# One encoder layer with routed experts on one core: mixing and experts in one overlaid block, and another order of the splits inside an expert block

## The chip, the cores and the metric

The kernel runs on one core of a Trainium2 chip. The metric is the device time of one execution in microseconds (us), the median of the runs; before, three runs gave 1725.3, 1727.06 and 1738.86 us. A profile is one further execution. PE is TensorE, DVE VectorE, ACT ScalarE, POOL GpSimd and SP SyncE. SP issues DMAs on one queue, POOL on another; both run on the core's 16 DMA engines.

## The reference

Two sequences (512 and 1024 tokens of width 1024, in all 1536 tokens, 12 tiles of 128) go through one layer: a retention mixer and a latent attention side by side, one output projection with residual, and a mixture of 32 experts (4 groups of 8; top group, then the top 2 experts in it). What follows the attention is what the change touches:

```
x = x + mix @ w_out
h = rmsnorm(x, g_ffn)
g = argmax(softmax(h @ w_rg)); top 2 of softmax(h @ w_re) inside group g; share = p_group * p_top / sum(p_top)
for each block of 128 rows of one expert e:
    y = (silu(xb @ w_g[e]) * (xb @ w_u[e])) @ w_d[e]        # w_g, w_u: 1024x512, w_d: 512x1024, f32
x[token] += share * y
out = rmsnorm(x, g_final)
```

## The kernel before

Four phases follow each other: projection (names a_), latent attention (c_), mixing and routing (d_, `phase_mix`) and the experts (e_, `phase_experts`). Each has its own on-chip tensors and its own block of five instruction streams; at its end all engines meet at a barrier and its semaphores are cleared.

Every f32 product is done in three passes (lines 91 to 95): both operands are split into a high half, the value rounded by a cast on ScalarE, and a low half, the remainder by a subtraction on VectorE, and TensorE adds high x high, high x low and low x high.

**Mixing.** `phase_mix` splits w_out into d_w_hi and d_w_lo (8 slices of 128x1024, raw in d_stage) and then walks the 12 tiles by `pairs` (line 73: two tiles written out, a loop, two tiles written out). For each tile: project and add the residual (d_x, line 1735), normalise (d_h_sb, 1739), turn the rows (1639), router logits (1646), a chain of 11 small VectorE operations that picks group and experts (1747 to 1769), and one tile later the places in each expert's queue (`queue`, 1713 to 1726). POOL stores x_mid (1578) and h_rows (1581) and scatters each token's entry into `table`, which lists the rows of each expert (1590). The loop leaves VectorE idle while TensorE projects. Behind the last tile VectorE works out the gates and then counts blocks: which expert each further block has, and n_pairs, the number of pairs of blocks (1792 to 1813). POOL stores the gates as `shares` (1598). SP has issued the whole first expert's weights behind its last tile (1553).

**Experts.** An expert's gate, up and down weights are six pieces j = 0 to 5 of 128x2048 f32, 1 MB each (0 and 1 gate, 2 and 3 up, 4 and 5 down), in the single buffer `raw`. SP loads a piece once its low half of the block before is done:

```
for j in pieces:
    sp.wait_ge(s_wlo[j], n)
    sp.dma_start(raw[:, j // 2, span(j)], w_exp[j // 2][e][:, span(j)]).then_inc(s_raw[j], 16)
```

Its order is pieces 0 to 3 of block n, then 4 and 5 of block n - 1. There are 32 blocks here. `each_block` (1876) writes out blocks 0 and 1 and loops over the rest. Block n on each engine:

- TensorE (2035): gate product (e_pg), up product (e_pu), turning of block n+1's rows (e_px, 1998), first half of the output product of block n-1 (e_py), turning of block n's gated product (e_ph, 2028), second half of e_py.
- ScalarE (2088): high halves of pieces 0 and 1, high half of the turned rows (2069), pieces 2 and 3, output scaling of block n-2 (2076), pieces 4 and 5 of n-1, high half of e_ph (2086), silu (2102).
- VectorE (2154): low halves of pieces 0 and 1 (2125), gated product of n-1 (`hidden`, 2146), low half of the turned rows (2132), pieces 2 and 3, output scaling (2139), low half of e_ph (2150), pieces 4 and 5 of n-1.
- POOL (1970): gather of block n+2's rows (e_xg, 1938), list of rows of block n+3 (e_who, 1932); then it waits until the scatter of block n-2 has landed, reads the code list of block n (e_code, 1978), gathers its shares (e_gate, 1946) and issues the scatter-add of block n-1's output into x_mid (1955). All of it waits in order on POOL.

At the end x_mid is read back and normalised (2112 to 2184).

Of the kernel before, what the change touches and what calls it, by code (L numbers as in the profile page):

```python
# [28 lines left out]
P = 128  # L29
D = 1024  # L30
# [1426 lines left out]
def phase_mix(nc, mixT, x_all, w_out, w_fold, g_ffn, w_rg, w_re, ident_d, route_d, blocks_d, x_mid, h_rows, table,  # L1457
              gates, blocks, n_pairs, s_tick, s_tock, raw, s_raw0, w_exp, shares):
    with ExitStack() as ctx:
        def sb(name, shape, dt=F32):  # L1460
            return ctx.enter_context(nc.sbuf_tensor("d_" + name, shape, dt))

        sems = phase_sems(nc, ctx)

# [3 lines left out]
        ident = sb("ident", [P, P])  # L1468
        route = sb("route", [P, 2 * NE + 2 * P])
        e_id, e_grp = route[:, 0:NE], route[:, NE:2 * NE]  # L1470
        before, ones = route[:, 2 * NE:2 * NE + P], route[:, 2 * NE + P:]
        stage = sb("stage", [P, 3, D])
        w_hi, w_lo = sb("w_hi", [P, KD, D], F32R), sb("w_lo", [P, KD, D], F32R)
        w_r = sb("w_r", [P, KD, NG + NE])
        g_row = sb("g_row", [P, D])
        eps = sb("eps", [P, 1])
        mx, xr = sb("mx", [P, 2, D]), sb("xr", [P, 2, D])
        mT_hi, mT_lo = sb("mT_hi", [P, 2, D], F32R), sb("mT_lo", [P, 2, D], F32R)
        x2, h_sb, hT = sb("x2", [P, 2, D]), sb("h_sb", [P, 2, D]), sb("hT", [P, D])
        junk = sb("junk", [P, D], BF16)  # L1480
        ssq, root, rstd = sb("ssq", [P, 1]), sb("root", [P, 1]), sb("rstd", [P, 1])
        g8, g8max, e8 = sb("g8", [P, 8]), sb("g8max", [P, 8]), sb("e8", [P, 8])
        g8i, e8i = sb("g8i", [P, 8], U32), sb("e8i", [P, 8], U32)
        gf, ef = sb("gf", [P, 1]), sb("ef", [P, 2])
        mask, pen, lem = sb("mask", [P, NE]), sb("pen", [P, NE]), sb("lem", [P, NE])
        hot = sb("hot", [P, 3, NE])
        seen = sb("seen", [P, NE])
        prod = sb("prod", [P, NE])
        place, spot = sb("place", [P, 2]), sb("spot", [P, 2])
        spot_i = sb("spot_i", [P, 2, 2], I32)  # L1490
        entry = sb("entry", [P, 2, 2, 2], I32)
        empty = sb("empty", [P, NE * ROWS // P * 2], I32)
        glog, elog = sb("glog", [P, TILES, NG]), sb("elog", [P, TILES, 2])
        gm, gz, ge, gd, gr = (sb(n, [P, TILES]) for n in ("gm", "gz", "ge", "gd", "gr"))
        gx = sb("gx", [P, TILES, NG])
        many_i, many, incl = sb("many_i", [P, NE], I32), sb("many", [P, NE]), sb("incl", [P, NE])
        step_no = sb("step_no", [P, MORE + AHEAD])
        upto, uses = sb("upto", [P, MORE + AHEAD, NE]), sb("uses", [P, MORE + AHEAD, NE])
        who, gone, base = (sb(n, [P, MORE + AHEAD]) for n in ("who", "gone", "base"))

        po = [ctx.enter_context(nc.psum_tensor(f"d_po{i}", [P, 1024], F32)) for i in range(2)]
        pt = ctx.enter_context(nc.psum_tensor("d_pt", [P, 1024], F32))
        pr = ctx.enter_context(nc.psum_tensor("d_pr", [P, 512], F32))
        pp = ctx.enter_context(nc.psum_tensor("d_pp", [P, 512], F32))
# [10 lines left out]
        s_spare, s_gates = sem("spare"), sem("gates")  # L1515
        s_d, s_q, s_gexp, s_count, s_g = sem("d"), sem("q"), sem("gexp"), sem("count"), sem("g")

        block = ctx.enter_context(nc.Block())

        @block.sync  # L1520
        def _(sp):
# [27 lines left out]

            pairs(sp, TILES, tile)  # L1550

            for j in range(6):
                sp.dma_start(raw[:, j // 2, raw_span(j)], w_exp[j // 2][0][:, raw_span(j)]).then_inc(s_raw0[j], 16)

        @block.gpsimd
        def _(pool):
# [28 lines left out]
            def enter(t, half):  # L1585
# [3 lines left out]
                for c in range(2):  # L1589
# [6 lines left out]
            pool.wait_ge(s_gates, 1)  # L1596
            settle_waits(pool, s_tick)
            pool.dma_start(shares[0:2 * ROWS, :].rearrange("(t p c) a -> p t (c a)", p=P, c=2),
                           gates[:]).then_inc(s_spare, 16)
# [3 lines left out]
            pool.wait_ge(s_spare, 16)  # L1603
# [52 lines left out]
        def _(act):  # L1656
# [12 lines left out]
            def tile(r, half, last):  # L1669
# [13 lines left out]
            pairs(act, TILES, tile)  # L1683
            act.wait_ge(s_gexp, 1)
# [4 lines left out]
        def _(dve):  # L1689
# [3 lines left out]
            dve.wait_ge(s_init, 3)  # L1693
            def split(t, half):
# [13 lines left out]
            def queue(t, half, again):  # L1708
# [6 lines left out]
                for c in range(2):  # L1715
                    ins = nc.vector.tensor_reduce(place[:, c:c + 1], pen[:] if c else prod[:], AX.X, ALU.add)
                queue_steps.chain(ins)
                queue_steps.chain(nc.vector.scalar_tensor_tensor(out=spot[:], in0=ef[:], scalar=float(ROWS),
                                                                 in1=place[:], op0=ALU.mult, op1=ALU.add))
# [556 lines left out]
```

## Time and profile before

| | us |
|---|---|
| three runs | 1725.3, 1727.06, 1738.86 |
| median | 1727.06 |
| the profiled execution | 1740.69 |
| its span, first to last instruction | 1739.2 |
| projection, about 0 to 497 | 497 |
| latent attention, about 497 to 798 | 301 |
| mixing and routing, about 798 to 1040 | 242 |
| experts and final norm, about 1040 to 1739 | 699 |

The span is read in stages, since the share of busy time over all of it mixes stages with different limits. Of a stage, the windows give the busy time of each engine, the granted TensorE clock and the share and rate of DMA. The chain is followed back from the last instruction to what released it each time; "idle before" of an instruction is the time in which its engine had nothing to run, with the releaser that ended it.

### The profile page before, as it was taken

The numbers are of one execution on the slowest core, as the hardware profiler recorded it, in microseconds if no ns is written. First come the engines' busy times: TensorE is split into PE (matmuls) and PEld (weight loads), VectorE is DVE, ScalarE is ACT, GpSimd is POOL, SyncE is SP. The second block draws the span as 40 slices with busy tenths as digits, with TensorE's granted clock in tenths as the row PEclk, the third lists the DMA queues.
The fourth block names the chain that finished last, engine by engine and source line by source line (L and its number), as shares of the span: only waits on it lengthen the run. The fifth ranks groups of instructions, "written<-read, shape, count | busy, mean of one in ns | idle before, by whom it ended". The sixth has DMA issues, their size and how long they took to land. (4 is left out here: it accounts for less than half of the span.)

```text
span 1739.2 us, 21978 instructions
## 1 busy us (share of the span) xinstructions
PE 1517.8 (87%) x7474; PEld 1251.4 (72%) x7474; DVE 1091.5 (63%) x1590; ACT 841.2 (48%) x1112; POOL 323.3 (19%) x291
## 2 busy tenths in 40 slices
PE   6999999999947799994999936999999989999980
PEld 5888788888836678872788825778777768777760
DVE  5656754434335577662355545888887878888854
ACT  6433433333324454452222215777766757767734
POOL 0000111111110000000012222223333333343340
PEclk9999999999967899996999967999999999999995
DMA  7132411221132100005344526999999999999947
GB/s 241 61 97 100 138 55 61 73 67 55 37 105 73 61 25 13 19 13 170 120 145 146 215 76 240 366 379 370 377 366 346 365 320 349 361 354 365 369 134 298
DMA packets 83266, 327.17 MB, mean 188 GB/s; under 512 B 16819, under 2 KB 27203, under 8 KB 58499
## 3 DMA queue, kind: packets, MB, share of 16 engines
q1 hardware_dynamic: 63426, 278.88, 43.4%
q0 software_dynamic: 19776, 47.47, 9.4%
q8 instruction: 37, 0.61, 0.1%
q14 instruction: 27, 0.21, 0.0%
HBM read 281.83 MB, written 53.91 MB: 193 GB/s over the span
## 5 line engine op out<-in xcount | busy, mean ns | idle before, releaser
L2125 DVE TENSOR_TENSOR e_w_lo<-raw,e_w_hi 128x2048 fp32r<-128x2048 f32 x192 | 428.0, 2282 | 8.5 <-ACT e_w_hi L2064 8.5
L2064 ACT CAST e_w_hi<-raw 128x2048 fp32r<-128x2048 f32 x192 | 356.8, 1912 | 14.3 <-PEq L104 12.7
L93 PE MATMUL a_p<-a_w_hi,a_xT_hi 128*128 128x512 f32 (+1 forms) x480 | 194.8, 406 | 3.4 <-DVE a_w_lo L679 3.3
L95 PE MATMUL a_p<-a_w_hi,a_xT_lo 128*128 128x512 f32 (+1 forms) x480 | 187.4, 390 | 0.0
L94 PE MATMUL a_p<-a_w_lo,a_xT_hi 128*128 128x512 f32 (+1 forms) x480 | 186.5, 389 | 0.0
L93 PE MATMUL e_py<-e_w_hi,e_hT_hi 128*128 128x512 f32 x256 | 108.3, 423 | 8.0 <-DVE e_w_lo L2125 8.0
L93 PEld LDWEIGHTS a_p<-a_w_hi,a_xT_hi 128*128 128x128 f32 x480 | 91.4, 190 | 20.4 <-DVE a_xT_lo L673 3.7
L93 PE MATMUL e_pg<-e_w_hi,e_xT_hi 128*128 128x512 f32 x256 | 102.5, 401 | 1.8 <-DVE e_xT_lo L2132 1.8
L95 PEld LDWEIGHTS a_p<-a_w_hi,a_xT_lo 128*128 128x128 f32 x480 | 91.1, 190 | 17.9
L93 PE MATMUL d_po<-d_w_hi,d_mT_hi 128*128 128x512 f32 x192 | 81.8, 426 | 24.8 <-DVE d_w_lo L1702 24.8
L94 PE MATMUL e_py<-e_w_lo,e_hT_hi 128*128 128x512 f32 x256 | 103.0, 402 | 0.0
L95 PE MATMUL e_py<-e_w_hi,e_hT_lo 128*128 128x512 f32 x256 | 102.7, 401 | 0.0
L94 PEld LDWEIGHTS a_p<-a_w_lo,a_xT_hi 128*128 128x128 f32 x480 | 91.6, 191 | 14.9
L95 PE MATMUL e_pg<-e_w_hi,e_xT_lo 128*128 128x512 f32 x256 | 102.1, 399 | 0.0
L94 PE MATMUL e_pg<-e_w_lo,e_xT_hi 128*128 128x512 f32 x256 | 102.0, 399 | 0.0
L95 PE MATMUL e_pu<-e_w_hi,e_xT_lo 128*128 128x512 f32 x256 | 101.2, 395 | 0.0
L93 PE MATMUL e_pu<-e_w_hi,e_xT_hi 128*128 128x512 f32 x256 | 101.1, 395 | 0.0
L94 PE MATMUL e_pu<-e_w_lo,e_xT_hi 128*128 128x512 f32 x256 | 101.0, 395 | 0.0
L2076 ACT ACTIVATE e_y_sb<-e_py,e_gate 128x512 f32<-128x512 f32 x32 | 22.0, 688 | 138.4 <-PE e_py L95 80.8
L1946 POOL DMA_INDIRECT e_gate<-s_shares,e_code x32 | 59.6, 1863 | 157.9 <-DMA e_code<-s_table 146.1
L1431 DVE TENSOR_TENSOR c_pT_lo<-c_pt,c_pT_hi 128x512 fp32r<-128x512 f32 x80 | 52.2, 683 | 47.8 <-ACT c_pT_hi L1282 47.8
L2150 DVE TENSOR_TENSOR e_hT_lo<-e_ph,e_hT_hi 128x512 fp32r<-128x512 f32 x32 | 22.1, 692 | 95.1 <-ACT e_hT_hi L2086 95.1
(310 smaller groups left out, 3306.2 us busy)
## 6 DMA issues: line engine op xcount, KB each, us to landing
raw<-in_w_gate SPq DMA_DIRECT2D x64, 1024.0 KB
raw<-in_w_up SPq DMA_DIRECT2D x64, 1024.0 KB
raw<-in_w_down SPq DMA_DIRECT2D x64, 1024.0 KB
a_x_sb<-in_x SPq DMA_DIRECT2D x24, 512.0 KB, 4.0
s_mid<-a_kv SPq DMA_DIRECT2D x12, 512.0 KB, 2.9
a_kv<-s_mid SPq DMA_DIRECT2D x12, 512.0 KB, 3.5
d_mx<-s_mixT SPq DMA_DIRECT2D x12, 512.0 KB, 5.4
d_xr<-in_x SPq DMA_DIRECT2D x12, 512.0 KB, 3.7
```

The costliest lines, as they stand in the source:

```text
L93: pe.matmul(out, st_hi, mv_hi, start=first, stop=False)
L94: pe.matmul(out, st_hi, mv_lo, start=False, stop=False)
L95: return pe.matmul(out, st_lo, mv_hi, start=False, stop=last)
L1431: nc.vector.tensor_tensor(pT3_lo[:, 4 * i:4 * i + 4, j * P:(j + 1) * P], pt[:, c * 512:(c + 1) * 512].rearrange("p (k i) -> p k i", k=4), ...
L1946: pool.indirect_dma_start(out=gate[half][:], out_offset=None, in_=shares, in_offset=bass.IndirectOffsetOnAxis(ap=code[half][:, 1:2], axis= ...
L2064: nc.scalar.copy(w_hi[:, j // 2, span(j)], raw[:, j // 2, span(j)]).then_inc(s_whi[j], 1)
L2076: nc.scalar.activation(y_sb[half][:, 0:512], py[:, 0:512], ACT.Copy, scale=gate[half][:, 0:1]).then_inc(s_ya, 1)
L2125: nc.vector.tensor_tensor(w_lo[:, j // 2, span(j)], raw[:, j // 2, span(j)], w_hi[:, j // 2, span(j)].bitcast(F32), ALU.subtract).then_inc ...
L2150: nc.vector.tensor_tensor(hT_lo[:], ph[:], hT_hi[:].bitcast(F32), ALU.subtract).then_inc(s_hlo, 1)
```

## The change

Mixing and experts share one block of instruction streams: no barrier and no clearing of semaphores lies between them. For that all on-chip tensors of both lie in two arenas, `split` for the halves and `plain` for the rest, with places that overlap where one is dead before the other is written, and PSUM is one tensor `acc`. In rows of the changed kernel's order everything has these three names. New waits guard the overlap: SP issues expert 0's weights in two parts (pieces 0 to 2 behind tile 1, once w_out is split; 3 to 5 behind tile 10); VectorE waits for the cleared table before it splits w_out.

The splits of expert 0's pieces 0 to 3 move into the tail of mixing. Block 0 of the experts no longer has them. The count of blocks moves behind block 0's turned rows. POOL's clearing of e_xg is dropped, that of e_gate and the store of the shares move behind the first gathers. Inside each expert block, piece 1 is split behind the gated product and the turned rows.

```diff
+                if isinstance(r, int) and t in (1, TILES - 2):
+                    sp.wait_ge(s_wlo, KD)
+                    for j in range(3) if t == 1 else range(3, 6):
+                        sp.dma_start(raw[:, j // 2, raw_span(j)],
+                                     w_exp[j // 2][0][:, raw_span(j)]).then_inc(ex.s_raw[j], 16)
             pairs(sp, TILES, tile)
-            for j in range(6):
-                sp.dma_start(raw[:, j // 2, raw_span(j)], w_exp[j // 2][0][:, raw_span(j)]).then_inc(s_raw0[j], 16)
...
+                if last:
+                    act.wait_ge(s_po, TILES)
+                    ex.upper(nc.scalar, 0, 0)
                 for b in range(2):
                     act.wait_ge(s_ht, 2 * t + b + 1)
...
             pairs(act, TILES, tile)
+            for j in range(1, 4):
+                ex.upper(nc.scalar, j, 0)
...
+            dve.wait_ge(s_tab[1], 16)
...
+                if last:
+                    dve.wait_ge(s_x2, TILES)
+                    ex.lower(nc.vector, 0, 0)
                 if not (isinstance(t, int) and t == 0):
                     queue(t - 1, 1 - half, not (isinstance(t, int) and t == 1))
+                if last:
+                    ex.lower(nc.vector, 1, 0)
...
             nc.vector.tensor_copy(prod[:, 0:1], spot[:, 0:1]).then_inc(s_spot, 1)
+            ex.lower(nc.vector, 2, 0)
+            ex.lower(nc.vector, 3, 0)
...
+            eng.wait_ge(ex.s_pairs, 1)
             with eng.Fori(1, pair_count(eng)) as r:
...
         def _(sp):
-            sp.dma_start(ident[:], ident_d).then_inc(s_const, 16)
+            sp.wait_ge(s_normed, TILES)
             sp.dma_start(g_row[:], g_final.partition_broadcast(P)).then_inc(s_const, 16)
...
-            for half in range(2):
-                nc.gpsimd.memset(gate[half][:], 0.0)
-                nc.gpsimd.memset(xg[half][:], 0.0).then_inc(s_clear, 1)
-            pool.wait_ge(s_clear, 2)
             for n in range(2):
                 list_rows(n, start_of(n))
             for half in range(2):
                 gather_rows(0, half)
             pool.wait_ge(s_xg[0], 16)
             list_rows(0, start_of(2))
+            for half in range(2):
+                ins = nc.gpsimd.memset(gate[half][:], 0.0)
+            ins.then_inc(s_clear, 1)
+            pool.wait_ge(s_clear, 1)
+            pool.wait_ge(s_gates, 1)
+            settle_waits(pool, s_tick)
+            pool.dma_start(shares[0:2 * ROWS, :].rearrange("(t p c) a -> p t (c a)", p=P, c=2),
+                           gates[:]).then_inc(ex.s_shares, 16)
+            pool.wait_ge(ex.s_shares, 16)
...
             def step(r, half):
                 n = 2 * r + half
-                split(0, n)
-                split(1, n)
-                if not (isinstance(r, int) and n == 0):
+                again = not (isinstance(r, int) and n == 0)
+                if again:
+                    split(0, n)
                     hidden(n - 1)
                 rows_lo(n)
-                split(2, n)
-                split(3, n)
+                if again:
+                    split(1, n)
+                    split(2, n)
+                    split(3, n)
+                else:
+                    count_blocks(dve)
```

ScalarE's step has the same new order: piece 0, turned rows, pieces 1 to 3. `ex.upper` and `ex.lower` are the split of one piece on ScalarE and VectorE, with the waits of before.

What stands in a row on VectorE in one block of the experts' loop, before:

```order
L2125 TENSOR_TENSOR e_w_lo<-raw,e_w_hi 128x2048 x2
L2146 TENSOR_TENSOR e_h_sb<-e_act_g,e_pu 128x512
L2131 ISA
L2132 TENSOR_TENSOR e_xT_lo<-e_px,e_xT_hi 128x512
L2131 REGISTER_ALU
L2132 TENSOR_TENSOR e_xT_lo<-e_px,e_xT_hi 128x512
L2125 TENSOR_TENSOR e_w_lo<-raw,e_w_hi 128x2048 x2
```

and after (L1537 is the low half of a piece, L2222 the gated product, L2208 the turned rows):

```order
L1537 TENSOR_TENSOR split<-plain,split 128x2048
L2222 TENSOR_TENSOR plain<-plain,acc 128x512
L2207 ISA
L2208 TENSOR_TENSOR split<-acc,split 128x512
L2207 REGISTER_ALU
L2208 TENSOR_TENSOR split<-acc,split 128x512
L1537 TENSOR_TENSOR split<-plain,split 128x2048 x3
```

One piece has moved from ahead of the gated product to behind the turned rows.

VectorE behind the last queue places of mixing, before (L1776 is the last copy of the queue places, L1778 begins the gates, L1792 the count of blocks, L1807 to L1813 its end, L2125 pieces 0 and 1 of block 0):

```order
L1776 COPY d_prod<-d_spot 128x1
L1778 TENSOR_REDUCE d_gm<-d_glog 128x12
...
L1789 TENSOR_TENSOR gates<-d_gr,d_gd 128x12
L1792 TENSOR_SCALAR d_many_i<-d_pp 128x32
...
L1813 TENSOR_SCALAR n_pairs<-d_many_i 1x1
...
L2125 TENSOR_TENSOR e_w_lo<-raw,e_w_hi 128x2048 x2
L2132 TENSOR_TENSOR e_xT_lo<-e_px,e_xT_hi 128x512 x2
L2125 TENSOR_TENSOR e_w_lo<-raw,e_w_hi 128x2048 x4
```

and after (L1867 is the last copy, L1871 begins the gates, L1888 to L1909 is the count):

```order
L1867 COPY plain<-plain 128x1
L1537 TENSOR_TENSOR split<-plain,split 128x2048 x2
L1871 TENSOR_REDUCE plain<-plain 128x12
...
L1882 TENSOR_TENSOR plain<-plain 128x12
...
L2208 TENSOR_TENSOR split<-acc,split 128x512 x2
L1888 TENSOR_SCALAR plain<-acc 128x32
...
L1909 TENSOR_SCALAR plain<-plain 1x1
L1537 TENSOR_TENSOR split<-plain,split 128x2048
```

Pieces 2 and 3 stand ahead of the gates, and the count stands behind the turned rows of block 0.

POOL at the phase end, before (entries of the last tile, shares, clearing, first lists and gathers):

```order
L1590 DMA s_table<-d_entry,d_spot_i 49152x2 x4
L1598 DMA s_shares<-gates 128x12x2
...
L1960 MEMSET e_gate 128x1
L1961 MEMSET e_xg 128x1024
L1960 MEMSET e_gate 128x1
L1961 MEMSET e_xg 128x1024
L1932 DMA e_who<-s_table 128x2 x2
L1938 DMA e_xg<-s_h_rows,e_who 128x1024 x2
L1932 DMA e_who<-s_table 128x2
```

and after:

```order
L1674 DMA s_table<-plain 49152x2 x4
L2000 UNCONDITIONAL_BRANCH
L2010 DMA plain<-s_table 128x2 x2
L2016 DMA plain<-s_h_rows,plain 128x1024 x2
L2010 DMA plain<-s_table 128x2
L2044 MEMSET plain 128x1 x2
L2049 DMA s_shares<-plain 128x12x2
```

The lists and gathers follow the entries, and the store of the shares has moved behind them.

## Rows read from the trace of the kernel before

**Rows 1.** Windows: us, busy PE PEld DVE ACT POOL, PEclk, DMA share, GB/s.

```profile
798.00:1040.00 242.00, 190.95 (x914) 157.79 (x914) 113.47 (x420) 53.10 (x84) 40.67 (x55) 0.85 0.45 153
1040.00:1072.00 32.00, 16.08 (x60) 12.97 (x61) 13.72 (x9) 13.95 (x10) 10.11 (x13) 0.63 0.53 184
...
1100.00:1260.00 160.00, 157.82 (x724) 127.41 (x723) 141.74 (x96) 118.38 (x95) 54.28 (x41) 1.00 1.00 374
1260.00:1660.00 400.00, 375.45 (x1685) 299.96 (x1684) 328.19 (x222) 272.01 (x221) 141.80 (x101) 0.99 0.97 355
```

**Rows 2.** Page, part 4: the chain of work that ended last, by engine.

```profile
DMA 22%; issue 5%; PE 3%; DVE 3%; ACT 3%; POOLq 2%; POOL 1%; DVEq 0%; ACTq 0%; SPq 0%
```

**Rows 3.** Timeline of POOL across the phase end: start, duration, line, operation, idle before.

```profile
1028.60 0.97 POOL L1590 DMA_INDIRECT s_table<-d_entry,d_spot_i  x1 [0.30 <-issue]
...
1040.18 0.10 POOL L1960 MEMSET e_gate<- 128x1 f32 x1 [9.51 <-POOLq L104]
```

**Rows 4.** Timeline of DVE in the last mixing tile and across the phase end.

```profile
1020.21 0.16 DVE L1747 COPY d_glog<-d_pr 128x4 f32<-128x4 f32 x1 [2.19 <-PE d_pr L1646]
...
1035.12 0.13 DVE L1813 TENSOR_SCALAR n_pairs<-d_many_i 1x1 int32<-1x1 int32 x1
1040.25 0.06 DVE L2142 MEMSET e_eps<- 128x1 f32 x1 [5.00 <-PEq L104]
```

**Rows 5.** Chain in order of time, first block of the experts: start, duration, what.

```profile
1042.38 2.37 DMA e_who<-s_table
...
1045.70 8.69 DMA e_xg<-s_h_rows,e_who
...
1057.86 0.79 PE e_pg L93
```

**Rows 6.** Timeline of SP's queue: the expert weights issued in the first blocks.

```profile
1044.50 2.53 SPq L1892 DMA_DIRECT2D raw<-in_w_gate  x2
...
1071.17 2.54 SPq L1892 DMA_DIRECT2D raw<-in_w_gate  x2
```

**Rows 7.** Chain in order of time: one block of the scatter chain, and the last scatter.

```profile
1259.59 10.49 DMA s_x_mid<-e_y_sb,e_code
...
1271.44 4.70 DMA e_code<-s_table
...
1279.42 10.21 DMA s_x_mid<-e_y_sb,e_code
...
1697.07 6.27 DMA s_x_mid<-e_y_sb,e_code
```

**Rows 8.** Timeline of POOL: scatters of blocks 0, 5 and 29.

```profile
1098.38 1.66 POOL L1955 DMA_INDIRECT s_x_mid<-e_y_sb,e_code  x1 [13.46 <-DVE e_y_sb L2139]
...
1193.35 3.76 POOL L1955 DMA_INDIRECT s_x_mid<-e_y_sb,e_code  x1 [0.30 <-issue]
...
1672.96 1.65 POOL L1955 DMA_INDIRECT s_x_mid<-e_y_sb,e_code  x1 [0.30 <-issue]
```

**Rows 9.** Timeline of DVE: one expert block of the even stretch.

```profile
1155.50 0.69 DVE L2150 TENSOR_TENSOR e_hT_lo<-e_ph,e_hT_hi 128x512 fp32r<-128x512 f32 x1 [2.16 <-ACT e_hT_hi L2086]
1156.11 8.89 DVE L2125 TENSOR_TENSOR e_w_lo<-raw,e_w_hi 128x2048 fp32r<-128x2048 f32 x4
1164.91 0.68 DVE L2146 TENSOR_TENSOR e_h_sb<-e_act_g,e_pu 128x512 f32<-128x512 f32 x1
1165.51 1.28 DVE L2132 TENSOR_TENSOR e_xT_lo<-e_px,e_xT_hi 128x512 fp32r<-128x512 f32 x2
...
1174.18 0.69 DVE L2150 TENSOR_TENSOR e_hT_lo<-e_ph,e_hT_hi 128x512 fp32r<-128x512 f32 x1 [2.33 <-ACT e_hT_hi L2086]
```

**Rows 10.** Waits in 1258 to 1660: who waits for whom; total, times, longest.

```profile
PE e_ph L2028 <- DVE e_h_sb L2146: 21.2, 19, 4.1
...
ACT e_y_sb L2076 <- DMA e_gate<-s_shares,e_code: 21.9, 4, 9.0
```

**Rows 11.** Waits in 1109 to 1258: ScalarE for the gate weights.

```profile
ACT e_w_hi L2064 <- DMA raw<-in_w_gate: 0.9, 2, 0.5
```

More of the change, by code:

```diff
@@ L1454, with raw_span, __init__, at @@
 NOWHERE = 1 << 20
-def phase_mix(nc, mixT, x_all, w_out, w_fold, g_ffn, w_rg, w_re, ident_d, route_d, blocks_d, x_mid, h_rows, table,
-              gates, blocks, n_pairs, s_tick, s_tock, raw, s_raw0, w_exp, shares):
+def raw_span(j):
+    return slice(2048 * (j % 2), 2048 * (j % 2 + 1))
+KB = 1024
+SPLIT_WORDS, PLAIN_WORDS = 27648, 25536
+class Map:
+    def __init__(self, arena, start):
+        self.arena, self.next = arena, start
+    def at(self, shape, dt, offset):
+        count = 1
+        for n in shape[1:]:
+            count *= n
+        words = count * (2 if dt == BF16 else 4) // 4
+        view = self.arena[0:shape[0], offset // 4:offset // 4 + words]
+        if dt not in (F32, F32R):
+            view = view.bitcast(dt)
+        if len(shape) == 3:
+            return view.rearrange("p (a b) -> p a b", a=shape[1])
+        if len(shape) == 4:
+            return view.rearrange("p (a b c) -> p a b c", a=shape[1], b=shape[2])
+        return view
+    def add(self, shape, dt=F32):
+        count = 1
+        for n in shape[1:]:
+            count *= n
+        offset = self.next
+        self.next += (count * (2 if dt == BF16 else 4) + 31) // 32 * 32
+        return self.at(shape, dt, offset)
@@ L1497, in phase_mix @@
[L1497 to L1504, printed above, removed]
+        w_r = sb([P, KD, NG + NE])
@@ new lines, in phase_mix @@
+        entry = sb([P, 2, 2, 2], I32)
+        glog, elog = sb([P, TILES, NG]), sb([P, TILES, 2])
+        gm, gz, ge, gd, gr = (sb([P, TILES]) for _ in range(5))
+        gx = sb([P, TILES, NG])
+        many_i, many, incl = sb([P, NE], I32), sb([P, NE]), sb([P, NE])
+        step_no = sb([P, MORE + AHEAD])
+        who, gone, base = (sb([P, MORE + AHEAD]) for _ in range(3))
+        po = [acc[:, 1024 * i:1024 * (i + 1)] for i in range(2)]
+        pt = acc[:, 2048:3072]
+        pr, pp = acc[:, 3072:3584], acc[:, 3584:4096]
@@ L1514, in phase_mix @@
         s_tab = [sem("tab0"), sem("tab1")]
-        s_spare, s_gates = sem("spare"), sem("gates")
+        s_gates = sem("gates")
+        s_steps = sem("steps")
         s_d, s_q, s_gexp, s_count, s_g = sem("d"), sem("q"), sem("gexp"), sem("count"), sem("g")
-        block = ctx.enter_context(nc.Block())
         @block.sync
@@ L1812, in _ @@
             nc.vector.tensor_copy(n_pairs[:, 0:1], many_i[0:1, 0:1])
-            tail.chain(nc.vector.tensor_scalar(n_pairs[:, 1:2], many_i[0:1, 0:1], -1.0, None, ALU.add))
-def raw_span(j):
-    return slice(2048 * (j % 2), 2048 * (j % 2 + 1))
-def phase_experts(nc, w_exp, ident_d, h_rows, table, shares, blocks, n_pairs, s_tick, raw, s_raw, x_mid, g_final,
-                  out):
+            nc.vector.tensor_scalar(n_pairs[:, 1:2], many_i[0:1, 0:1], -1.0, None, ALU.add).then_inc(ex.s_pairs, 1)
@@ L1825, in phase_experts @@
+        return s_h, s_gates, count_blocks
+def phase_experts(nc, block, sems, split, plain, acc, ex, w_exp, h_rows, table, shares, s_tick, x_mid, g_final, out, gates, s_normed, s_gates,
+                  count_blocks):
     KF = FE // P
     with ExitStack() as ctx:
-        def sb(name, shape, dt=F32):
-            return ctx.enter_context(nc.sbuf_tensor("e_" + name, shape, dt))
-        sems = phase_sems(nc, ctx)
         def sem(name):
             return phase_sem(nc, sems, "e_" + name)
-        ident = sb("ident", [P, P])
@@ L1846, in phase_experts @@
[L1846 to L1848 removed]
+        ident, w_hi, w_lo, raw = ex.ident, ex.w_hi, ex.w_lo, ex.raw
+        who, code, xg, y_sb, gate = ex.who, ex.code, ex.xg, ex.y_sb, ex.gate
+        xT_hi, xT_lo, act_g, h_sb = ex.xT_hi, ex.xT_lo, ex.act_g, ex.h_sb
+        hT_hi, hT_lo, g_row, eps = ex.hT_hi, ex.hT_lo, ex.g_row, ex.eps
```

183 lines of the change are left out of this document (101 added, 82 removed).

## The prediction

> **What bounds the kernel now.** I read the windows first, then the chain that ended last, then the timelines of single engines at two places.
>
> The windows [rows 1] show four regimes behind the latent phase. In mixing (798 to 1040) the DMA share is 0.45 and TensorE is busy 191 of 242 us. From 1040 to 1072 everything is thin: TensorE 16 of 32 us, clock 0.63, DMA 0.53. From 1100 to 1260 DMA and TensorE are both full (share 1.00, 374 GB/s, TensorE 157.8 of 160 us). From 1260 to 1660 DMA stays near full (0.97, 355 GB/s), but TensorE has 24.6 us of holes.
>
> The chain [rows 2] is a DMA chain: 22% of the span, against 3% for each compute engine. Its links in the experts [rows 7] are the scatter-add of a block's output rows into x_mid (10.49 us to land), then the code list of the block after next (4.70 us), whose queueing waited for that landing, then the gather of the shares, then the next scatter, 19.83 us after the first (1259.59 to 1279.42). POOL issues all of these itself, one behind the other. After block 0, where POOL waited 13.46 us for the output, it starts a scatter with 0.30 us of idle time in front of it [rows 8], so the outputs lie ready and the chain waits only for its own transfers. Its pace is (1193.35 - 1098.38) / 5 = 19.0 us a block at first and (1672.96 - 1193.35) / 24 = 20.0 us after that [rows 8].
>
> The compute side needs less. VectorE's cycle in the even stretch is 1174.18 - 1155.50 = 18.7 us [rows 9]. In that cycle the gated product (L2146) stands behind four weight pieces (8.89 us), and the turning of h, the second half of the output product and the next scaling follow on it. So two loops run side by side: one of compute at 18.6 us and one of transfers at 19 to 20 us. The second sets the end.
>
> **Part 1: the phase end goes.** Before, the table entries of tile 11 are issued at 1028.60 [rows 3]. VectorE then counts blocks until 1035.25, the barrier and the clearing of semaphores last to 1040.25 [rows 4], and POOL clears two 128x1024 tiles. The first list of rows is read at 1042.38 [rows 5]. After the change POOL reads it as soon as the entries have landed. The trace has no landing time for that scatter, so I bound it: a list of the same 1 KB lands in 2.37 us [rows 5], the last scatter of 128 whole rows in 6.27 us [rows 7]. That gives 1031.0 to 1034.9. I take 2.9 us, near the small transfer, thus 1031.5.
>
> What is new ahead of it are four weight pieces. On VectorE a low half costs 8.89 / 4 = 2.2 us [rows 9]. Piece 0 fits between the normalised rows of tile 11 and the queue places of tile 10, where VectorE had nothing to do. Piece 1 falls into the 2.19 us idle ahead of the logits of tile 11 [rows 4], but its high half on ScalarE has to wait for the copies of the turned rows, so I charge 0.5 us to the routing. Pieces 2 and 3 stand behind the entries, ahead of the gates (4.4 us), and the gates' store moves behind the first row gathers; nobody needs the shares until block 0's output, for which POOL waits 13.46 us in any case [rows 8]. The block count goes behind the first turned rows of block 0 and lies beside TensorE's gate and up products, 1057.86 to beyond 1071.17 [rows 5, 6]. Cost of both: nothing; if that cover were gone, at most the 6.7 us from the entries to the end of the count (1028.60 to 1035.25, [rows 3, 4]). The list thus goes out at 1032.0 against 1042.38: -10.4 us, with bounds -7.0 and -10.9.
>
> The following steps keep their length, except for company. The first gather took 8.69 us [rows 5] with two pieces issued at 1044.50 beside it [rows 6]. Now pieces 0 and 1 of expert 1 are long in and 2 and 3 are ending. The gather may gain up to 2.4 us (8.69 against the 6.27 of a transfer alone), and the list may lose up to 2.3 us (4.70 under load against 2.37, [rows 5, 7]). I take zero for the pair and keep both ends.
>
> The early loads themselves (3 MB behind tile 1, 3 MB behind tile 10) lie in a stretch with DMA share 0.45 [rows 1]. 3 MB at 374 GB/s are 8.4 us, the 242 us hold 12 tiles, and a tile's inputs are asked for a tile ahead. Cost: nothing; uncovered, at most those 8.4 us once. Two waits are new. VectorE waits for the cleared table behind its constants, ahead of weights that come later still. SP waits for the last normalised rows before the final scale row, and behind it stand only pieces that have to wait for VectorE anyway. I take nothing for either. POOL's wait for the gates holds the rows of block 2 and block 0's shares, both with more than 10 us to spare [rows 8].
>
> Does the weight stream also win more than these 10.4 us? Expert 2 can be loaded only when piece 0 of expert 1 has been split, and that needs block 0's gate product done. Before, it goes out at 1071.17 [rows 6]; it moves by the same amount as that product. So the stream gets no second gain. Part 1: -10.4 us, -13.3 to -4.7.
>
> **Part 2: product and turned rows ahead of piece 1.** In each expert block VectorE now runs three pieces, product, rows, three pieces. The product is free 2.2 us earlier. TensorE waited for it 21.2 us in 19 blocks of the late stretch [rows 10], 1.1 us each. In the even stretch TensorE is full already [rows 1], so the compute loop can shorten by about half a microsecond there and by about one later. But it isn't the loop that ends last: with scatters started after 0.30 us of idle time [rows 8], outputs that lie ready earlier wait longer. I take 0 us. The best case is that the late stretch runs at the early pace: 24 x 1.0 = -24 us. The worst within this mechanism is that the compute loop runs ahead sooner and the late pace begins at once: 5 x 1.0 = +5 us.
>
> The Trainium skill (DMA: Bandwidth & Descriptors, Queues, rings and completion order) says that each DMA engine goes round the queues that have work, packet by packet. By that rule a scatter is as slow as the weight queue is non-empty, and the order of the splits doesn't matter; the trace agrees as far as it goes, with 10.49 us beside weights and 6.27 us alone [rows 7].
>
> **Sum.** 1740.7 (span 1739.2 and 1.5 around it) - 10.4 - 0 = 1730.3 us for the profiled execution. That execution lies 13.6 us above the median, 1727.06; where, one profile can't show, but the pace of the scatter chain is the part that can vary. The difference carries over to the median: 1716.7, and I say 1716 us.
>
> **Rivals.**
> (a) The experts speed up as well. The late stretch moves 355 GB/s where the early one moved 374 [rows 1], so there is room; with pieces 4, 5, 0 and 1, 2, 3 in even groups the compute loop recovers faster after a late share (9.0 us at most, [rows 10]) and the queue is filled more evenly. Half to all of -24 us: 1692 to 1704, taken as 1699. Against it stands that POOL never waits for compute. The Trainium skill (DMA: Bandwidth & Descriptors, Bandwidth) gives about 358 GB/s as one core's share of HBM. By that rule the late stretch is at its ceiling and this rival is worth nothing; the trace disagrees, with 374 GB/s over 160 us [rows 1].
> (b) The start gives little. The list or the first gather is held by the weight pieces now in flight, or the entries land late: -4.7 us, and the chain runs at the late pace from the start, +5: no change, 1727.
> (c) Slower: piece 1 starves the stream. Its low half now ends behind product (0.6), rows (1.2) and about 0.6 us of waiting for its high half, 2.4 us later, and SP issues in order, so pieces 2 and 3 of the next expert can't pass it. If the queue runs dry there each time, every block pays. The loss outweighs part 1 from 10.4 / 31 = 0.34 us a block. A third of the 2.4 us, 0.8 x 31 = 25, gives 1727 - 10 + 25 = 1742. Against it: in the stretch where DMA is fullest ScalarE waited for gate weights twice, 0.9 us in all [rows 11], and piece 1 now has 2.4 us more to land.
>
> **Chances.** Forecast 0.50, (a) 0.24, (b) 0.17, (c) 0.09. A measurement tells about 1% from no change, 17 us: faster is below 1710, slower above 1744. The forecast lies 6 us inside "same"; with the 14 us that the three runs of before spread, about a fifth of it falls beyond 1710. Faster: 0.10 + 0.24 less a bit = 0.32. Slower: part of (c) and little else, 0.06. The rest, 0.62, is same. The range takes in most of (a) and all of (b): 1695 to 1734.
>
> **What would show it.** Right: the first list of rows about 10 us sooner behind the last table entries, no 5 us gap on any engine, the weights of expert 1 in flight ahead of the first gate product; TensorE's wait for the product gone; the scatters still 19 to 20 us apart with 0.30 us idle ahead. Wrong for (a): scatters 19 us apart or less in the late stretch. Wrong for (c): ScalarE waiting for pieces of weights, DMA share below 0.95. Part 1 is wrong if the entries' landing, or the first gather with weights beside it, takes up the time that the barrier left.

## The result and the profile after

The changed kernel takes 1775.95 us (median of 4 runs, 1771.44 to 1785.33) against 1732.96 us of the kernel before on the same chip: ratio 1.0247, 95% interval 1.0203 to 1.0291. It is slower by 43 us, and the forecast of 1716 with its range of 1695 to 1734 was wrong. Here and in the later tables the ratios and intervals leave out single executions that ran over 1.5% longer than the fastest of their kernel (two of e5, one of e6), while the medians in us take in all.

Windows of the changed kernel, as in [rows 1] (span, busy time and count of PE, PEld, DVE, ACT, POOL, granted clock, DMA share, GB/s):

```profile
798.00:1040.00 242.00, 187.40 (x914) 157.51 (x914) 116.10 (x407) 60.31 (x88) 46.09 (x57) 0.84 0.51 174
1040.00:1072.00 32.00, 28.94 (x121) 23.33 (x122) 21.97 (x30) 17.73 (x15) 8.73 (x12) 0.86 0.47 147
1100.00:1260.00 160.00, 147.83 (x673) 122.26 (x672) 133.18 (x89) 107.25 (x87) 51.93 (x39) 0.97 0.98 360
1260.00:1700.00 440.00, 385.36 (x1681) 315.79 (x1679) 330.09 (x221) 273.72 (x222) 143.77 (x102) 0.93 0.91 318
```

The thin stretch from 1040 to 1072 is filled (TensorE 28.9 of 32 us, before 16.1). The loss is behind it: the late stretch moves 318 GB/s where it moved 355, and it lasts longer.

The start, in the timeline of POOL (start, duration, instruction, in brackets the idle time before it and what ended it):

```profile
1023.06 2.42 POOL L1674 DMA_INDIRECT s_table<-plain  x1 [5.00 <-DVE plain L1867]
1025.78 1.90 POOL L1674 DMA_INDIRECT s_table<-plain  x1 [0.30 <-issue]
1033.41 1.16 POOL L2010 DMA_DIRECT2D plain<-s_table  x2 [5.74 <-DMA s_table<-plain]
1036.32 1.05 POOL L2016 DMA_INDIRECT plain<-s_h_rows,plain  x1 [1.75 <-DMA plain<-s_table]
...
1085.91 3.63 POOL L2033 DMA_INDIRECT s_x_mid<-plain  x1 [19.57 <-DVE plain L2215]
```

The first list of rows goes out at 1033.41 (before 1042.38, [rows 5]) and the first scatter at 1085.91 (before 1098.38, [rows 8]): 12.5 us won. Then the chain of scatters loses it. The one at 1189.90 is the last of its early pace of 20.8 us a block; from there to the one at 1707.31 lie 24 blocks, 21.6 us each. Before, it was 19.0 and 20.0. And 0.30 us of idle time stands ahead of each scatter from 1260 to 1660 (5.4 us for 18, below): the outputs lie ready, POOL doesn't wait for them. The chain that ended last, as in [rows 2]:

```profile
DMA 31%; PE 11%; issue 6%; ACT 2%; POOLq 2%; DVE 2%; POOL 1%; SPq 0%; ACTq 0%; DVEq 0%
DMA s_x_mid<-plain 21%; DMA plain<-s_table 8%; PE acc L93 3%; PE acc L95 3%; PE acc L94 3%; POOLq L2007 1%; PE acc L1725 1%; POOL plain L2024 1%; ACT plain L2194 1%; ACT split L1531 1%; DVE split L1537 0%; DMA plain<-s_w_fold 0%; ACT plain L1763 0%; PE acc L1718 0%; DMA s_table<-plain 0%
```

It is the same chain of scatter and code list with a larger share. The waits from 1100 to 1700 (engine, tile and line, what it waited for, us in total, times, longest):

```profile
ACT split L2144 <- PE acc L2079: 111.9, 38, 6.5
...
PE acc L2079 <- DMA plain<-s_h_rows,plain: 64.3, 23, 5.2
```

TensorE's wait for the product, 21.2 us in [rows 10], has almost gone (2.5 us in two waits), as forecast. In its place TensorE waits 64.3 us for gathered rows (L2079), and ScalarE with it at the turned rows (L2144). These gathers are issued by POOL, behind its scatters. So what has slowed POOL's chain? All of POOL's indirect DMAs from 1260 to 1660, kernel before (count, busy, mean ns):

```profile
L1955 POOL DMA_INDIRECT s_x_mid<-e_y_sb,e_code x21 | 42.4, 2020 | 6.3 <-issue 6.3
L1938 POOL DMA_INDIRECT e_xg<-s_h_rows,e_who x20 | 40.8, 2041 | 6.1 <-issue 6.1
L1946 POOL DMA_INDIRECT e_gate<-s_shares,e_code x20 | 36.5, 1822 | 98.5 <-DMA e_code<-s_table 98.5
```

and the changed kernel:

```profile
L2033 POOL DMA_INDIRECT s_x_mid<-plain x18 | 45.2, 2511 | 5.4 <-issue 5.4
L2024 POOL DMA_INDIRECT plain<-s_shares,plain x18 | 37.5, 2081 | 98.2 <-DMA plain<-s_table 91.6 <-issue 6.6
L2016 POOL DMA_INDIRECT plain<-s_h_rows,plain x19 | 25.9, 1366 | 5.8 <-issue 5.8
```

On the chain POOL's own instructions have become longer: a scatter 2.5 us instead of 2.0, a gather of shares 2.1 instead of 1.8. The gather of rows has become shorter, 1.4 instead of 2.0; it stands beside the landing of the scatter and isn't a link of the chain. The landing of a scatter, from its start, went from a median of 10.7 to 12.3 us.

### The profile page after: what moved, and what is told of

Its sections match the earlier page's. It is cut to its first block, busy times and chain, and to the rows that moved or that the text cites. A ratio compares the mean times of both kernels' runs of the same rounds, so it can differ in the third digit from the quotient of the medians.

```text
span 1774.9 us, 21982 instructions
## 1 busy us (share of the span) xinstructions
PE 1522.5 (86%) x7474; PEld 1269.8 (72%) x7474; DVE 1095.7 (62%) x1590; ACT 841.5 (47%) x1112; POOL 323.1 (18%) x289
## 4 chain that ended last, share of the span: by engine, by line
DMA 31%; PE 11%; issue 6%; ACT 2%; POOLq 2%; DVE 2%; POOL 1%; SPq 0%; ACTq 0%; DVEq 0%
DMA s_x_mid<-plain 21%; DMA plain<-s_table 8%; PE acc L93 3%; PE acc L95 3%; PE acc L94 3%; POOLq L2007 1%; PE acc L1725 1%; POOL plain L2024 1%; ACT plain L2194 1%; ACT split L1531 1%; DVE split L1537 0%; DMA plain<-s_w_fold 0%; ACT plain L1763 0%; PE acc L1718 0%; DMA s_table<-plain 0%
## 5 line engine op out<-in xcount | busy, mean ns | idle before, releaser
L1537 DVE TENSOR_TENSOR split<-plain,split 128x2048 fp32r<-128x2048 f32 x192 | 428.4, 2285 | 17.9 <-ACT split L1531 17.8
L93 PE MATMUL acc<-split 128*128 128x512 f32 x960 | 397.6, 414 | 34.9 <-DVE split L1788 24.3
L95 PE MATMUL acc<-split 128*128 128x512 f32 x960 | 389.0, 405 | 0.0
L94 PE MATMUL acc<-split 128*128 128x512 f32 x960 | 388.7, 405 | 0.0
L1531 ACT CAST split<-plain 128x2048 fp32r<-128x2048 f32 x192 | 356.4, 1910 | 0.3 <-DMA plain<-in_w_gate 0.3
L93 PEld LDWEIGHTS acc<-split 128*128 128x128 f32 x960 | 191.3, 199 | 77.8 <-issue 28.5
L95 PEld LDWEIGHTS acc<-split 128*128 128x128 f32 x960 | 188.9, 197 | 41.8
L94 PEld LDWEIGHTS acc<-split 128*128 128x128 f32 x960 | 190.0, 198 | 38.1
L2079 PE MATMUL acc<-plain 128*128 128x128 f32 x264 | 45.8, 328 | 81.8 <-DMA plain<-s_h_rows,plain 81.8
L2079 PEld LDWEIGHTS acc<-plain 128*128 128x128 f32 x264 | 38.7, 200 | 92.3 <-DMA plain<-s_h_rows,plain 91.6
L2144 ACT CAST split<-acc 128x512 fp32r<-128x512 f32 x64 | 35.6, 589 | 134.6 <-PE acc L2079 134.5
L2024 POOL DMA_INDIRECT plain<-s_shares,plain x32 | 60.0, 1876 | 162.7 <-DMA plain<-s_table 149.5
L2033 POOL DMA_INDIRECT s_x_mid<-plain x32 | 82.1, 2565 | 34.3 <-DVE plain L2215 25.3
L2226 DVE TENSOR_TENSOR split<-acc,split 128x512 fp32r<-128x512 f32 x32 | 22.1, 692 | 99.7 <-ACT split L2161 99.6
```

Of the source, the lines that this page charges most:

```text
L93: pe.matmul(out, st_hi, mv_hi, start=first, stop=False)
L94: pe.matmul(out, st_hi, mv_lo, start=False, stop=False)
L95: return pe.matmul(out, st_lo, mv_hi, start=False, stop=last)
L1531: eng.copy(self.w_hi[:, j // 2, cols], self.raw[:, j // 2, cols]).then_inc(self.s_whi[j], 1)
L1537: eng.tensor_tensor(self.w_lo[:, j // 2, cols], self.raw[:, j // 2, cols], self.w_hi[:, j // 2, cols].bitcast(F32), ALU.subtract).then_inc ...
L2024: pool.indirect_dma_start(out=gate[half][:], out_offset=None, in_=shares, in_offset=bass.IndirectOffsetOnAxis(ap=code[half][:, 1:2], axis= ...
```

## First experiments: which part costs

Two parts were exchanged one by one, and the two moves of the new order were taken apart. In the changed kernel (in short, the order of one block on VectorE):

```diff
 # e1, VectorE (ScalarE: 0, 1, rows, 2, 3)
-    split(0), hidden, rows_lo, split(1), split(2), split(3)
+    split(0), split(1), hidden, rows_lo, split(2), split(3)
 # e3, VectorE (ScalarE: 0, 1, rows, 2, 3)
+    split(0), hidden, split(1), rows_lo, split(2), split(3)
 # e4, VectorE (ScalarE as changed: 0, rows, 1, 2, 3)
+    split(0), rows_lo, split(1), hidden, split(2), split(3)
```

e2 is the kernel before with the changed order. Expected:

> The changed kernel with the old order of an expert block on ScalarE and VectorE (pieces 0, 1, product, turned rows, 2, 3); the shared block, the early loads and splits of expert 0 stay. Theory H (held): the loss is in the order. With the turned rows ahead of pieces 1 to 3, their splits wait for the gather of the rows, and the weight loads wait for the splits, so the weight queue runs dry once a block. H expects the scatters 20.0 us apart again, the start's 12 us kept: 1721 us, ratio 0.993 (0.988 to 0.998). Theory S (shared block): the loss comes from the overlay or the earlier start, whatever the order: 1770 us, ratio 1.02, scatters 21.5 us apart. Theory P (product): as H, but only the product's move matters; it expects here what H does.

> The kernel before with the new order alone (piece 0, product, turned rows, pieces 1, 2, 3 on VectorE; piece 0, turned rows, 1, 2, 3 on ScalarE). H: scatters 21.5 us apart, TensorE waits for the gathered rows some 60 us, DMA share near 0.91 in the late stretch: 1.5 x 30 = 45 us more than before, 1778 us, ratio 1.026. S: no loss from the order, ratio 1.000 (0.995 to 1.005). P: as H.

> The changed kernel with the product ahead of piece 1 but the turned rows behind it, as before (VectorE: 0, product, 1, rows, 2, 3; ScalarE: 0, 1, rows, 2, 3). H: pieces 2 and 3 still stand behind the rows as they did before, piece 1 no longer: 1721 us, ratio 0.993, scatters 20.0 us apart. P: still 1770 us. S: still 1770 us.

> The changed kernel with the turned rows ahead of piece 1 but the product behind it (VectorE: 0, rows, 1, product, 2, 3; ScalarE: 0, rows, 1, 2, 3). H: nothing gained back, 1770 to 1785 us, ratio 1.02 to 1.03 (the product is later than in either kernel). P: 1721 us, ratio 0.993. S: 1770 us.

Measured, each against the kernel before on the same chip (1731.37 us):

| kernel | us | ratio | 95% |
|---|---|---|---|
| e1, shared block, old order | 1722.48 | 0.9949 | 0.9932 to 0.9965 |
| e2, old block, new order | 1780.67 | 1.0287 | 1.0270 to 1.0305 |
| e3, product ahead alone | 1754.72 | 1.0125 | 1.0101 to 1.0149 |
| e4, rows ahead alone | 1807.12 | 1.0431 | 1.0413 to 1.0448 |

e1 and e2 settle the first question. The shared block is worth -8.9 us, the order +49.3 us, together +40.4 against the 43.0 measured. Theory S falls. But e3 fits neither H (1721) nor P or S (1770): one harmless-looking move costs 32 us with pieces 2 and 3 behind the rows as ever. H and P do not say why.

The traces show what varies. e3's scatters, 1260 to 1660, take 3.07 us each:

```profile
L2033 POOL DMA_INDIRECT s_x_mid<-plain x19 | 58.3, 3068 | 6.2 <-issue 6.2
```

Now POOL beside VectorE, in the changed kernel. First POOL, then VectorE:

```profile
1529.59 0.56 POOL L2061 DMA_DIRECT2D plain<-s_table  x1 [9.06 <-issue]
1535.67 2.55 POOL L2024 DMA_INDIRECT plain<-s_shares,plain  x1 [5.52 <-DMA plain<-s_table]
1538.52 2.50 POOL L2033 DMA_INDIRECT s_x_mid<-plain  x1 [0.30 <-issue]
1541.33 1.28 POOL L2016 DMA_INDIRECT plain<-s_h_rows,plain  x1 [0.30 <-issue]
```

```profile
1525.60 6.68 DVE L1537 TENSOR_TENSOR split<-plain,split 128x2048 fp32r<-128x2048 f32 x3
1532.21 0.68 DVE L2222 TENSOR_TENSOR plain<-plain,acc 128x512 f32<-128x512 f32 x1
1532.81 1.28 DVE L2208 TENSOR_TENSOR split<-acc,split 128x512 fp32r<-128x512 f32 x2
1535.00 6.70 DVE L1537 TENSOR_TENSOR split<-plain,split 128x2048 fp32r<-128x2048 f32 x3 [0.92 <-ACT split L1531]
```

A low half takes 2.2 us, so the train (subtractions back to back) that starts at 1535.00 has its borders near 1537.2, 1539.4 and 1541.7. The gather of shares starts at 1535.67, 1.5 us ahead of a border, and takes 2.55 = 1.5 + 1.05. The scatter starts 0.9 us ahead of the next, and takes 2.50 = 0.9 + 1.65 or so. The gather of rows starts some 0.3 us ahead of the train's end, and takes 1.28. With no subtraction running, a gather takes 1.05 us and a scatter 1.65. So an indirect DMA waits for the subtraction that VectorE is in, and gets in at its end. It is no single case: of the 96 indirect DMAs that start behind 1040 in the changed kernel's trace, 80 start while such a subtraction runs, and each of the 80 has its own 1.05 or 1.65 us left at the end of that one. VectorE doesn't pay: all its 128x2048 subtractions take 2.27 to 2.32 us, before and after, also those that start while a scatter runs. The plain list read at 1529.59 lies in the middle of the train before and takes 0.56 us as always: it does not wait. The same place in the kernel before:

```profile
1538.67 2.69 POOL L1946 DMA_INDIRECT e_gate<-s_shares,e_code  x1 [4.76 <-DMA e_code<-s_table]
1541.66 1.66 POOL L1955 DMA_INDIRECT s_x_mid<-e_y_sb,e_code  x1 [0.30 <-issue]
```

```profile
1531.55 8.89 DVE L2125 TENSOR_TENSOR e_w_lo<-raw,e_w_hi 128x2048 fp32r<-128x2048 f32 x4
1540.35 0.68 DVE L2146 TENSOR_TENSOR e_h_sb<-e_act_g,e_pu 128x512 f32<-128x512 f32 x1
1540.95 1.28 DVE L2132 TENSOR_TENSOR e_xT_lo<-e_px,e_xT_hi 128x512 fp32r<-128x512 f32 x2
```

There a train had four pieces. The gather of shares waited for the end of the fourth, and the scatter then fell onto the turned rows, which read one operand from PSUM: 1.66 us. The old order thus has a gap behind the longest train, and a scatter whose gather waited for the train's end falls into it. So it is with 8 of the 20 scatters that start from 1260 to 1660, and with 3 more neither the gather nor the scatter met a piece. The new order has trains of three and three: 14 of its 18 gathers in that stretch wait in the first piece of a train, get in at an inner border, and their scatters wait in the second. One scatter of the 18 takes 1.65 us. That it is the operand in PSUM which lets POOL in was so far only a reading; the third round tests it.

The Trainium skill (SBUF — State Buffer, Who interferes with whom) states this as a lock: a VectorE instruction with two SBUF inputs contends with a GpSimd instruction that reads SBUF, and the loser blocks for the whole instruction. For whole pieces the rows agree as far as POOL is the loser; VectorE isn't seen to lose. Of tensor_tensor and the issue of a DMA the same section says that an earlier probe saw none, which the 2.50 us here contradict for indirect DMAs and the 0.56 us bear out for plain ones.

e4 is another case. Its scatters take 1.65 us throughout, its gathers of shares still 2.1, and POOL waits for VectorE's scaling of the output:

```profile
L2033 POOL DMA_INDIRECT s_x_mid<-plain x18 | 29.8, 1654 | 84.2 <-DVE plain L2215 69.2 <-issue 15.1
```

And TensorE waits for the product:

```profile
PE acc L2109 <- DVE plain L2222: 48.7, 18, 2.7
```

With the product behind rows and piece 1, the loop of compute has become the bound, at 22.2 us a block (its scatters are 21.9 and 22.5 us apart in turn). H's price for it, 1770 to 1785, was 22 us too low.

## Second: change the length of the subtraction, not the order

If POOL waits for the rest of a subtraction, shorter ones let it in sooner. In the changed kernel (e5, e6) and in the shared block with the old order (e7, e8), with k = 2 or 4 (operands shortened):

```diff
+        w = 2048 // k
+        for i in range(k):
+            cols = slice(raw_span(j).start + i * w, raw_span(j).start + (i + 1) * w)
+            ins = eng.tensor_tensor(w_lo[..cols], raw[..cols], w_hi[..cols], ALU.subtract)
+        ins.then_inc(self.s_wlo[j], 1)
```

> The changed kernel with each low half of a weight piece taken in 2 subtractions of 128x1024 instead of one of 128x2048. Theory D (door): a row gather or scatter of POOL can begin its work only when the VectorE subtraction that is running ends. In the traces its duration is 1.65 us (scatter) or 1.05 us (gather) where none runs, and that plus what is left of the running one (up to 2.2 us) inside a train of them. The new order made the trains three and three long instead of four and two and moved the scatter into them, so that it takes 2.5 us instead of 1.65, and the chain on POOL grows. D expects here: scatters of 1.65 to about 2.8 us, mean near 2.1 instead of 2.56; share gathers down by some 0.5 us; 1.2 us a block less: 1745 us, ratio 1.008 (1.000 to 1.015). Theory Q (queue): POOL's instruction is long because the DMA rings are full of weights, and the chain is slow for the same reason; the size of the subtractions doesn't matter: 1776 us or, for the added fixed cost, 1785, ratio 1.025 to 1.03, scatters 2.5 us.

> The same with 4 subtractions of 128x512. D: at most 0.55 us is left to wait for, scatters near 1.9 us, 1.7 us a block less than the changed kernel: 1725 us, ratio 0.997 (0.985 to 1.01); VectorE pays 18 x 0.06 = 1.1 us a block for the cuts, which may show in the early stretch. Q: 1790 us, ratio 1.035.

> The shared block with the old order of the splits (1722 us, 0.995) and 2 subtractions a piece. D: its late stretch runs at 20.1 us a block since there too scatters fall into trains now and then; it comes nearer to the 18.7 us of its early stretch: 24 x 0.7 = 17 us less, 1705 us, ratio 0.985 (0.975 to 0.992). Q: no gain, 1722 to 1730 us, ratio 0.995 to 1.000.

> The same with 4 subtractions a piece. D: 24 x 1.0 = 24 us less, 1698 us, ratio 0.981 (0.970 to 0.992), unless VectorE, with 1.1 us more a block, becomes the bound. Q: 1722 to 1735 us, ratio 0.995 to 1.003.

| kernel | us | ratio | 95% |
|---|---|---|---|
| e5, new order, halves | 1739.38 | 1.0015 | 0.9978 to 1.0052 |
| e6, new order, quarters | 1715.60 | 0.9880 | 0.9830 to 0.9931 |
| e7, old order, halves | 1707.97 | 0.9847 | 0.9815 to 0.9878 |
| e8, old order, quarters | 1717.58 | 0.9908 | 0.9879 to 0.9937 |

More instructions for the same work, and all four medians are below those of their kernel with whole pieces (e8's, 0.9908 against e1's 0.9949, with intervals that overlap a little). Q falls by e5, e6 and e7. D's times held within 6 us for e5 and e7; e6 came out 9 us better and e8 20 us worse than priced. D's durations held less well: e5's scatters were to take 2.1 us and no more than about 2.8, and from 1260 to 1660 they take 3.0, since three of the 19 take about 8 us. So part of e5's time came out right by luck. In e7 the chain that ended last is no longer one of transfers:

```profile
DVE 17%; PE 17%; ACT 9%; issue 5%; DMA 4%; SPq 0%; DVEq 0%; POOL 0%; ACTq 0%; POOLq 0%
```

e8 shows the other side (its gathers of shares take 3.6 us there), and e6 shows it most clearly. One of e6's gathers of rows, POOL's row and then VectorE's:

```profile
1400.30 6.75 POOL L2019 DMA_INDIRECT plain<-s_h_rows,plain  x1 [0.30 <-issue]
```

```profile
1398.83 7.31 DVE L1539 TENSOR_TENSOR split<-plain,split 128x512 fp32r<-128x512 f32 x12
```

The gather starts 1.5 us into a train of twelve, is not let in at the next border nor at the eight behind it, and ends at 1407.05, 0.9 us behind the train. In other cases with the same cut it gets in after one piece, in others after a few. Whole pieces let POOL in at the first border in every trace here; cut ones sometimes keep it out to the end. What decides it isn't settled.

## Third: take the second SBUF operand away

The direct test keeps length, number and order of the instructions, and changes only where one operand lies (`open` is a cleared, unused 128x512 part of PSUM, read four times; operands shortened). It takes nothing off, so a low half holds the whole value again, and f1 and f2 don't compute the layer; they serve for the time alone:

```diff
-        eng.tensor_tensor(w_lo[..cols], raw[..cols], w_hi[..cols], ALU.subtract)
+        eng.tensor_tensor(w_lo[..cols], raw[..cols], self.open.unsqueeze(1).broadcast_to([P, 4, 512]), ALU.subtract)
```

f3 is the kernel before with pieces cut in halves.

> The changed kernel, whole pieces, but inside the expert blocks the low half of a piece is taken as raw minus a cleared part of PSUM instead of raw minus the high half: the same 128x2048 in one instruction, with one operand in SBUF instead of two. The low halves, and so the outputs, hold other values; the work in instructions is the same. Theory D (door): only subtractions with two SBUF operands keep POOL out. All gathers take 1.05 us and all scatters 1.65 us, the chain needs no more than 18.7 us a block, and the new order is no longer slower than the old: 1770 - 31 x 2.5 = 1695 us, ratio 0.98 (0.970 to 0.988). Theory L (length): any long VectorE instruction keeps POOL out, or it is the phase of the weight loads against the chain: scatters still 2.5 us, 1770 us, ratio 1.02.

> The same subtraction with one SBUF operand, in the shared block with the old order of the splits (0.995 with two). D: 1.05 and 1.65 us throughout, 18.7 us a block, ratio 0.98 (0.970 to 0.985), within 0.5% of the new order. If the order itself holds loads back, beside the door, this one is faster than the new order by over 1%. L: 1722 us, ratio 0.995, as with two operands.

> The kernel before with each low half of an expert's piece taken in 2 subtractions of 128x1024, nothing else. D: the same 1.0% as the shared block with the old order gained from it (0.9949 to 0.9847): 1714 us, ratio 0.990 (0.983 to 0.996). L: no gain or a loss by the fixed cost, ratio 1.000 to 1.005.

| kernel | us | ratio | 95% |
|---|---|---|---|
| f1, new order, one SBUF operand | 1702.05 | 0.9823 | 0.9773 to 0.9872 |
| f2, old order, one SBUF operand | 1703.40 | 0.9822 | 0.9775 to 0.9869 |
| f3, before, halves | 1717.78 | 0.9914 | 0.9885 to 0.9942 |

That decides it. (f3 gained 0.9% by the cut alone, as D had it.) Without the lock the two orders are equal: the 54 us between the changed kernel and e1 (1775.95 against 1722.48) have become 1.35 us the other way. The rows of f1 from 1260 to 1660:

```profile
L2041 POOL DMA_INDIRECT s_x_mid<-plain x22 | 36.3, 1651 | 15.5 <-DVE plain L2223 8.6 <-issue 6.9
L2032 POOL DMA_INDIRECT plain<-s_shares,plain x21 | 22.0, 1049 | 109.6 <-DMA plain<-s_table 102.8 <-issue 6.8
```

And one place of it, POOL and then VectorE:

```profile
1508.61 1.05 POOL L2032 DMA_INDIRECT plain<-s_shares,plain  x1 [5.98 <-DMA plain<-s_table]
1509.96 1.66 POOL L2041 DMA_INDIRECT s_x_mid<-plain  x1 [0.30 <-issue]
1511.92 1.04 POOL L2024 DMA_INDIRECT plain<-s_h_rows,plain  x1 [0.30 <-issue]
```

```profile
1508.14 6.68 DVE L1541 TENSOR_TENSOR split<-plain,acc 128x2048 fp32r<-128x2048 f32 x3 [0.53 <-ACT split L1532]
```

All three fall into a train of the same 6.68 us, and none waits; nor does any other of the 96 behind 1040. So neither the length of a VectorE instruction nor the phase against the weights was it. L falls. D's time for f1, 1695 us, was 7 us too good: many of its scatters are 19 to 20 us apart, with DMA share 0.95.

f1 also sizes the lock. Means over the blocks whose scatter starts from 1260 to 1660, in us:

| link of the chain | before | changed | f1 |
|---|---|---|---|
| scatter, instruction | 2.0 | 2.5 | 1.65 |
| its landing, from the end of the instruction | 8.75 | 9.65 | 8.5 |
| to the code list's issue | 1.4 | 1.4 | 1.4 |
| code list, to the gather of shares | 5.35 | 5.95 | 5.75 |
| gather of shares, instruction | 1.9 | 2.2 | 1.05 |
| to the next scatter | 0.3 | 0.3 | 0.3 |
| a block | 19.7 | 21.95 | 18.6 |

Waiting inside the two instructions is 2.0 us a block in the changed kernel and 1.2 before. It explains 0.8 of the 2.3 us that a block lost in this stretch. The other 1.5 us are landings: the scatter's (0.9) and the code list's (0.6). Of the 3.35 us that a block wins in f1, 2.0 are the instructions and 1.4 the landings. So the longer landings go, for the most part, when the lock goes; by which way they come wasn't tried.

One more order, the product alone ahead of piece 1, with halves:

> A try at more than 0.985: the shared block, pieces cut in 2 subtractions, and the product alone ahead of piece 1 (VectorE: 0, product, 1, rows, 2, 3; ScalarE: 0, 1, rows, 2, 3). With whole pieces this order gave 1.0125. With the old order in halves the chain that ended last had gone over to VectorE and TensorE, and TensorE waited 16.7 us in 20 blocks for the product. If the product's place is worth something once POOL is let in, 0.8 us a block: 1685 us, ratio 0.973. If a train of six halves without a break in front of the product keeps POOL out for its whole length now and then, as it did in the changed kernel with halves (8 us), the gain is lost: 1715 to 1740 us, ratio 0.99 to 1.00, with single gathers or scatters of over 5 us.

Measured: 1751.58 us, ratio 1.0113 (1.0041 to 1.0185). It is the second outcome in kind, with scatters of over 5 us, but 12 us beyond its range:

```profile
L2036 POOL DMA_INDIRECT s_x_mid<-plain x19 | 69.5, 3656 | 5.8 <-issue 5.8
```

Six of its scatters take 5.88 to 6.04 us, a train of four halves (4.6 us) and their own 1.65, less what had passed. So e7, the shared block with the old order and halves, is the fastest kernel here that computes the whole layer: 1.5% faster than the kernel before, of which the shared block alone gives 0.5% (e1).

## Why the prediction was wrong

**The windows and the chain** were read rightly: the end is set by POOL's chain of scatter, code list and gather, before and after.

**Part 1** held in its total. Priced at -10.4 us, it measured -8.9 us (e1, by its interval -12 to -6). Its inner terms were off: the entries took 7.6 us from the issue at 1025.78 to the list at 1033.41 and not 2.9, but VectorE handed them over earlier than assumed (the last entries issued 2.8 us earlier than before), and the first gather had landed when POOL went on at 1040.81, 4.5 us behind its start at 1036.32, and not in 8.69. Each went beyond its own bound, in opposite directions, so that the total came out right in part by luck.

**Part 2** is the step that failed: "I take 0 us", and with it the bounds of -24 and +5. The order cost 49 us where it stands alone (e2), and 53 in the shared block (the changed kernel against e1). Its reasons were that POOL never waits for compute and that the chain "waits only for its own transfers". The idle time ahead of a scatter, 0.30 us, said so, but idle time is only one of two places in which a wait can stand. The other is the instruction's own duration, and it stood in a group that the prediction quotes: the scatters of [rows 8] have 1.66, 3.76 and 1.65 us. The prediction took their starts and not their durations, and set the change of pace from 19.0 to 20.0 us at the very scatter that took 3.76. It left that change unexplained as something "that can vary". In the early stretch the scatters fell beside the trains, and from 1193.35 on about half of them into one (9 of the 20 that start from 1260 to 1660 take 2.5 us). With pieces in halves the same kernel has no such change: f3 holds 18.9 us a block over the same 24 blocks.

**TensorE's wait for the product** went, as forecast, and was worth nothing, as forecast: without the lock the two orders, f1 and f2, differ by 1.35 us.

**The rivals.** (c) had the sign and a DMA share below 0.95 (0.91), but not the mechanism: ScalarE waited for weights once, 0.3 us, and f1, with piece 1 in the same late place, runs at 1702 us. (a) took the late stretch for one that could recover, which is right (f1 does), but by another way than the order. The Trainium skill's rule on queues (DMA: Bandwidth & Descriptors, Queues, rings and completion order), by which the order of the splits would not matter, was weighed for the landing; the issue ahead of it, 2.5 us against 1.65, doesn't follow it. And the 358 GB/s that rival (a) was held against are, in the Trainium skill (DMA: Bandwidth & Descriptors, Bandwidth), what a core gets while the other core of its pair streams too; here one core runs, and the 374 GB/s of [rows 1] aren't at odds with that.

**The carry-over** from the profiled execution to the median isn't what made the forecast fail, but e1 shows that it isn't exact: its profiled execution is 18.8 us shorter than that of the kernel before (1721.88 against 1740.69), where the medians differ by 8.9.

## What to carry to other kernels

When one engine's instructions vary in duration with the same shape (1.65, 2.5, 3.7 us), ask before anything else what they wait for inside: put the starts beside what the other engines run, and look for borders. Where GpSimd issues indirect DMAs on the path that ends last, each VectorE subtraction with two SBUF operands is a wait of up to its own length, and moving such instructions changes which DMAs fall into them, even where a result that others wait for comes earlier. Cutting them in two gave 1.0% (e1 to e7) and 0.9% (f3) in the old order, and can also keep POOL out for longer (g1), so it has to be measured. One operand in PSUM gave more, but no kernel here does it and computes the layer; a gap left behind a train on purpose wasn't tried.

## What the runs showed of the hardware

- An indirect DMA's instruction on GpSimd waits for the running VectorE subtraction with two SBUF operands (2.2 us), then takes its 1.05 (gather) or 1.65 us (scatter). With one operand in PSUM it doesn't wait (none of 96 in f1, none of 96 in f2). A plain DMA of POOL, 0.55 to 0.62 us, doesn't wait either. The subtraction itself stays at 2.27 to 2.32 us.
- In trains of 128x1024 or 128x512 subtractions it is sometimes kept out to the train's end: up to 8.18 us for one scatter in e5 and 8.54 in e6, 6.75 us for many gathers in e6. In trains of 128x2048 no scatter or gather of these kernels took over 3.76 us.
- Landings differ too: from 1260 to 1660 a scatter of the changed kernel lands 9.65 us behind the end of its instruction, and 8.5 us in f1. The way from the one to the other is open.
